# Two more pairs of unread identity products on TensorE, inside the S5 outputs of a hybrid decoder step

## The reference, cut to what matters

```
bu_re = jnp.einsum('blgc,gpc->blgp', ug, bb_re)
...
_, _, h_re, h_im = lax.associative_scan(combine, (a_re, a_im, bu_re, bu_im), axis=1)
y = (jnp.einsum('gcp,blgp->blgc', c_re.astype(f32), h_re)
     - jnp.einsum('gcp,blgp->blgc', c_im.astype(f32), h_im)).reshape(bt, L, S5_WIDTH)
y = y + d_skip.astype(f32) * uf
g = jax.nn.gelu(y)
out = g * jax.nn.sigmoid(g @ w_glu.astype(f32))
```

## Time and profile before

| | us |
|---|---|
| three runs | 2810.78, 2817.34, 2817.27 |
| median | 2817.27 |
| the profiled execution, its own time | 2813.14 |
| its span in the trace | 2811.3 |

### The profile page before, as it was taken

How to read it: one execution, slowest core, us unless ns; L and a number is a source line. 1 busy time by engine, 2 the same in 40 slices (tenths; PEclk the granted TensorE clock), 3 DMA queues, 4 the chain that set the end, 5 groups by cost and what they waited for, 6 DMA issues and landing times.

```text
span 2811.3 us, 40640 instructions
## 1 busy us (share of the span) xinstructions
PE 2692.1 (96%) x16585; PEld 2564.1 (91%) x16585; DVE 1290.8 (46%) x1502; ACT 647.1 (23%) x948; POOL 996.6 (35%) x414
## 2 busy tenths in 40 slices
PE   8997999999999999999999999967999999999997
PEld 6975589999999999999999999967999999999997
DVE  4974654522222222275666766665352232222326
ACT  4012632300010001143333344342240011000102
POOL 2532334366676667410000000010524444443442
PEclk9996899999999999999999999988999999999998
DMA  4332021233333333314111112202101111111111
GB/s 143 102 89 65 1 92 45 107 135 132 130 142 112 142 120 134 129 56 151 67 55 67 71 69 75 78 31 78 53 31 46 46 45 45 45 45 45 49 49 70
DMA packets 89281, 223.89 MB, mean 80 GB/s; under 512 B 23031, under 2 KB 38552, under 8 KB 89000
## 3 DMA queue, kind: packets, MB, share of 16 engines
q1 hardware_dynamic: 70448, 178.98, 18.6%
q10 hardware_dynamic: 18712, 43.23, 4.1%
HBM read 163.41 MB, written 58.74 MB: 79 GB/s over the span
## 4 chain that ended last, share of the span: by engine, by line
PE 82%; DVE 11%; ACT 3%; issue 2%; POOL 1%; DMA 0%; DVEq 0%; ACTq 0%; SPq 0%; POOLq 0%
PE ps L343 49%; PE ps L352 7%; PE ps L1723 6%; PE ps L1784 4%; PE ps L423 3%; PE ps L456 3%; DVE lev L1850 3%; PE ps L470 2%; ACT lev L1977 2%; DVE ck L1850 1%; PE ps L1397 1%; DVE raw L1850 1%; PE ps L1824 1%; PE ps L1066 1%; DVE cum L1850 1%
## 5 line engine op out<-in xcount | busy, mean ns | idle before, releaser
L259 POOL TENSOR_TENSOR w_hi<-w_raw,ones 128x1024 fp32r<-128x1024 f32 x148 | 362.8, 2451 | 1614.2 <-PE ps L343 663.9
L343 PE MATMUL ps<-a_hi,w_hi 128*128 128x352 f32 x1896 | 613.3, 323 | 7.2 <-POOL w_lo L261 4.6
L343 PE MATMUL ps<-a_hi,w_lo 128*128 128x352 f32 x1896 | 611.5, 323 | 0.0
L343 PE MATMUL ps<-a_lo,w_hi 128*128 128x352 f32 x1896 | 609.5, 321 | 0.0
L261 POOL TENSOR_TENSOR w_lo<-w_raw,w_hi 128x1024 fp32r<-128x1024 f32 x148 | 378.3, 2556 | 11.6
L343 PEld LDWEIGHTS ps<-a_hi,w_hi 128*128 128x128 f32 x1896 | 356.7, 188 | 8.8 <-POOL w_lo L261 4.0
L343 PEld LDWEIGHTS ps<-a_lo,w_hi 128*128 128x128 f32 x1896 | 357.9, 189 | 0.0
L343 PEld LDWEIGHTS ps<-a_hi,w_lo 128*128 128x128 f32 x1896 | 357.8, 189 | 0.0
L716 ACT ACTIVATE sq<-ssq 128x1056 f32<-128x1056 f32 x64 | 69.7, 1088 | 1213.4 <-DVE ssq L681 1213.4
L343 PE MATMUL ps<-h_hi,w_hi 128*128 128x352 f32 x1056 | 342.1, 324 | 0.1
L343 PE MATMUL ps<-h_hi,w_lo 128*128 128x352 f32 x1056 | 340.1, 322 | 0.0
(11 more groups left out here) (294 smaller groups left out, 4379.2 us busy)
## 6 DMA issues: line engine op xcount, KB each, us to landing
w_raw<-w SPq DMA_DIRECT2D x156, 512.0 KB, 3.4
p_raw<-w SPq DMA_DIRECT2D x32, 512.0 KB, 4.4
w_hi_scratch<-p_hi SPq DMA_DIRECT2D x32, 512.0 KB, 2.7
w_lo_scratch<-p_lo SPq DMA_DIRECT2D x32, 512.0 KB, 3.6
w_hi<-w_hi_scratch SPq DMA_DIRECT2D x32, 512.0 KB, 4.0
w_lo<-w_lo_scratch SPq DMA_DIRECT2D x32, 512.0 KB, 4.8
x_scratch<-x ACTq DMA_DIRECT2D x16, 528.0 KB, 3.0
x<-x_scratch ACTq DMA_DIRECT2D x16, 528.0 KB, 7.6
```

What stands on the lines that cost most here:

```text
L259: pool.tensor_tensor(hi, whole, bc(ones[:, 0:P], 1, KC), ALU.mult).then_inc(hi_made, 1)
L343: mm = pe.matmul(tiles[:, t], wt[:, b, w], at_[:, k, cols], start=(n == 0 and i == 0), stop=(n == len(ks) - 1 and i == 2))
```

## The change

Inside `trio_out`, ahead of the wait for the third and the fourth quarter of states (`i` 8 and 12), and at `par` 0 only, TensorE waits until VectorE has read quarter 2 of the state inputs out of banks 0 and 1, and then issues two unread products into bank 0. The Toeplitz product of that `i` stands ahead of them.

```diff
@@ -1079,6 +1079,9 @@
                         out = ps[:, 4 + 2 * (g % 2) + par, (i - 3 * g) * NU:(i - 3 * g + 1) * NU]
                         pe.matmul(out, toep[:, par, i], u_c[:, 2 * i + par], start=True, stop=False)
                         if i % 4 == 0:
+                            if i >= 8 and par == 0:
+                                pe.wait_ge(v_read, 3)
+                                hold_clock(0, 2)
                             pe.wait_ge(h_ready, i // 4 + 1)
                         for r in range(2):
                             mm = pe.matmul(out, out_st[rows, r, i, 1:L].rearrange("p k c -> p (k c)"),
```

## The result

The changed kernel took 2797.19 us (median of 5 runs, 2794.71 to 2803.75), the kernel before 2817.27 us in the 5 runs beside them (2810.78 to 2817.53). The ratio is 0.9946, with a 95% interval of 0.9927 to 0.9964: faster by 15 us, between 10 and 21. Run again later, 12 times, it had a median of 2803.22 us and a ratio of 0.9966 (0.9950 to 0.9981), about 10 us by the ratio. Over all runs of this study the mean is 2814.0 us for the kernel before (49 runs, standard error 0.8) and 2801.5 us for the changed one (17 runs, 1.1), 12.5 us apart. Two slow executions of over 4400 us, one of the kernel before and one of e9, are left out everywhere.

A forecast was written before the change was run, and what follows sets the result against it. TensorE at half clock was taken to bound the S5 outputs, with the attention behind. The sum 10.8 + 0.9 + 2.0 = 13.7 us gave 2799.4 or 2803.6, so 2802 us was forecast, range 2794 to 2813.

The forecast's parts named there:

- C: Distance from the S5 outputs' first Toeplitz product to the gate's first product; the forecast gain of 13.7 us should reach it.
- The bound: S5 outputs from 227 us: TensorE bound at half clock, which fell after a 2.36 us wait for the third quarter.
- the dip in slices 3 to 5: The drop of granted clock on the profile page, in 70 us slices, placed around the S5 mixer and the attention.
- The first pair: Two unread products ahead of the third quarter's wait: 1.82 us, hidden by GpSimd's work, 0.6 us of idleness left.
- The new wait at the fourth quarter: At full clock TensorE reaches the fourth quarter early: a new 2.2 us gap, 1.82 us filled, 0.4 us idle.
- A: Distance from the S5 outputs' first Toeplitz product to the attention's first transpose; S5 outputs forecast to end 10.8 us earlier.
- The attention's start: First transposes and score products at full clock: 0.9 and 2.0 us less, so VectorE begins the attention at 248.0.
- B: Distance from the attention's first transpose to the first transposes of the prompt's probabilities; forecast terms there 0.9 and 2.0 us.
- What becomes of it behind: After the attention's start the clock falls as before, everything runs as before, and all 13.7 us reach the end.
- The rule of the Trainium skill: Activity releases the throttle, making the gain near nothing; set aside because TensorE, busy 227 to 263, stayed at 0.50.
- Rival A: Clock falls at the third quarter anyway; the second pair has no cover, 3.6 us slower, 2820.9 us; chance 0.08.
- the holding of the clock: With both pairs the clock stays full to the end of the S5 outputs; the forecast case, given 0.82.

The follow-up runs named there:

- e9: Changed kernel with e7's filled attention gaps, plus two unread products between the two blocks of transposes of the new positions; 2795.97 us, ratio 0.9938.
- e3: Changed kernel with only the two waits for v_read 3, without any unread product; 2815.83 us, measured once.
- e4: Changed kernel with one unread product instead of two in each place; 2825.55 us, measured once.
- e6: Changed kernel with needed Toeplitz products issued ahead of both waits in place of the unread pairs; 2799.94 us, ratio 0.9939.
- e1: Changed kernel with only the pair ahead of the third quarter; 2809.38 us, ratio 0.9986 to the kernel before.
- e2: Changed kernel with only the pair ahead of the fourth quarter; 2805.84 us, ratio 0.9983 to the kernel before.
- e10: Changed kernel with Toeplitz products plus one and five unread ones ahead of the waits, and the attention filled as in e9; 2785.84 us, ratio 0.9902.
- e7: Changed kernel with five unread products in each of TensorE's two gaps at the attention's start; 2796.12 us, ratio 0.9933.

## Why the prediction was right

**The forecast held, in size and by its steps.** I had 13.7 us from the trace; C is 13.6 us shorter. That they agree to 0.1 us is luck: with e3 in place of the kernel before, C would be 16.7 us shorter. The measured medians lie 20 us apart in the first set and 9 in the second; the means of all runs are 12.5 us apart, with a standard error of 1.4.

- **The bound.** That the half clock of 227 to 263 was due to the gap of 2.36 us is shown by e3 (the gap alone, same waits, same fall) against the changed kernel, and by e4 (less filled, same fall). e6 held it there without an unread product. The forecast places the dip in slices 3 to 5; its own windows put it into the fourth and fifth.
- **The first pair.** Priced at 1.82 us, hidden, with 0.6 us left: 0.59 in the trace.
- **The new wait at the fourth quarter.** It was the step most easily missed: a TensorE at full clock gets there early. e1 shows it and its price. Filled, 0.48 us was left against 0.4 forecast.
- **A.** 10.8 us forecast, 10.9 measured, with TensorE and GpSimd equally far apart at its start in both traces. **The attention's start**, 0.9 + 2.0 us: B is 2.8 us shorter. VectorE began 246.06 - 203.50 = 42.6 us behind the first Toeplitz product; the forecast's 248.0 - 205.42 is 42.6.
- **What becomes of it behind.** Nothing took it back: 10.9 + 2.8 = 13.7 us at the start of the prompt's transposes are 13.6 at the gate. The half clock of the attention came again, as forecast, and ended inside the same block of products (L1387 before, L1390 after). From VectorE's first `prob_s` to the end of the span it is 2811.3 - 261.68 = 2549.6 us before and 2795.4 - 246.06 = 2549.3 after, though 2553.0 in the second trace of the changed kernel.
- **The rule of the Trainium skill** that activity releases the throttle (page "TensorE: Matmul & The Clock Gate", section "What's actually happening"): I set it aside too broadly. The state steps did not bring the clock back in 13 us and more, but it came back over the unread products of e2 within 3.3 us, and in the kernel before over the products of the attention. That also changes a rival, below.

**Where a rival was mis-built.** Rival A said that with the clock down at the third quarter the second pair costs 3.6 us and gives nothing. e2 is that case: the 3.3 us are there, but the clock came back with them, and A was 3.7 us shorter instead of 3.6 longer. So the mechanism that I gave for the slower side did not show with two products, in the one trace of it; with one product it did (e4, A 1.7 us longer). The failed step is "then the S5 outputs run at half clock as now" behind the second pair. If it holds beyond that trace, the second pair also insures against a fall at the third quarter; it did not against the fall of e9.

**What was too sure.** I had given the holding of the clock 0.82 for the kernel as such. It is not a property of the kernel alone: e9 lost it 3 us behind a filled gap, with the same 0.6 and 0.5 us left as in the changed kernel. What decided it stays open. How often it happens is not known either: the runs without a trace don't say it, and a mean gain of 12.5 us (standard error 1.4) does not differ clearly from 13.7.

## What to carry to other kernels

Where TensorE waits for a chain of other engines inside a stretch of small products, the wait costs less than the half clock behind it: here 2.4 us of gap made 29 us of work take 1.8 times as long. Fill the gap, and then work out where the faster engine will wait next, since that gap needs filling too. Before filling with unread products, look for needed ones that can be issued ahead, and put products of one kind side by side.

## What the runs showed of the hardware that I had not expected

**What TensorE did before the clock rose.** In e2 it went from 0.50 to 1.00 over the four records of the unread pair (3.3 us), after 13.2 us of state steps in which it had not. In e9 it rose over the ten unread records at the attention's start. In e4 it did not rise over two unread records (1.9 us), nor over the state steps around them, though TensorE was never idle from 234 to 264 us. The same state steps kept 1.00 for 17.8 us in the kernel before. In the kernel before, the changed one and e3 it rose without an unread product, while TensorE was busy without a gap with the attention's products on `prob_st` (L1387, L1390 and L1389).

**What stood before it fell.** In the S5 outputs the clock fell at gaps of 2.4, 1.48 and 1.21 us (e1), but held over one of 1.17 us (e6, behind 12 Toeplitz records). It held over those of 0.5 to 0.6 us, but once fell 3 us behind one of 0.49 us (e9). So the length of the gap alone does not decide it. In the late attention it survived gaps of 1.1 and 1.4 us, as in the changed kernel, whose window from 310 to 350 us is at 1.00 with this in it (timeline of TensorE):

```profile
327.82 1.09 PE L1410 MATMUL ps<-ident,prob 128*128 128x128 f32 x8 [1.11 <-ACT prob_t L1556]
...
332.20 1.93 PE L1420 MATMUL ps<-prob_t,v_tok 128*64 128x512 f32 x4 [1.43 <-ACT prob_t L1556]
```

**State products side by side run at more than twice the rate.** 0.073 us a record in a block of 24 or 32, 0.165 in fours between Toeplitz products, both at full clock (e6, e10). In a block, products on rows 0 to 63 and on rows 64 to 127, into different banks, follow one another directly. The Trainium skill (page "TensorE: Matmul & The Clock Gate", section "Part 3: Packing small matmuls — row/col tiling") says that products on different row groups of the array run at the same time, which fits; no run here separated this from the absence of the Toeplitz products between them. Toeplitz products gain too: 12 records in 1.66 us, against two in 0.43 in the mix.

**The runs scatter as much ahead of the change as behind it.** The first Toeplitz product came at 205.42, 203.50, 201.13, 199.23, 199.37 and 211.93 us in the traces of before, changed, e1, e2, e3 and e4. One part is a single VectorE operation on the chain that ended last, the same in all kernels (line 967 in the changed kernel's trace: min, median and max in ns, start):

```profile
L967 DVE TENSOR_SCALAR turn<-turn x1: 3402/3402/3402, 161.4 to 161.4; 128x2048 f32<-128x2048 f32 x1
```

It took 3.40 us in this trace of the changed kernel, 1.40 in that of before and 1.24 in e2; I did not test what sets it. The other part goes with the clock: its mean from 160 to 200 us was 0.83 in the trace of before, 0.96 in the changed one, 1.00 in e2 and 0.70 in e4. Behind the attention, where no kernel was changed, it is no less: from the first product of the gate to the end of the span the traces take between 2440.2 us (e7) and 2452.5 us (e3). Of two kernels whose medians differ by some 10 us, the distances inside the traces tell more than the few runs do, and even they carry up to 3 us for the same work.
